# Reordered output steps, a PV product one head later, and earlier splits of weights and keys in a one-core attention and gating block

## The reference

```python
h = rmsnorm(x, norm_gain)
a_u, a_v, a_z, b_q, b_k, b_v, b_z, i_q, i_k, i_w = split_cols(h @ w_in, IN_SIZES)  # 3 x 512, 512, 64, 64, 512, 512, 64, 8
ya = spatial_gating(a_u, a_v, ...)           # gelu, layernorm of v, masked 128x128 mixing in blocks
q, k = rmsnorm(b_q per head, q_norm_gain), rmsnorm(b_k, k_norm_gain)
# per block of 128 queries (8 index heads, 8 attention heads, one shared k and v):
idx_score = sum over heads of relu(i_q . layernorm(i_k)) * i_w * scale
sel = top_k(where(admissible, idx_score, NEG), 256)     # ties: the earlier key
p = softmax(q . k[sel] * scale - slope[head] * |qpos - sel|, inadmissible = NEG)
yb = p @ v[sel]
# each branch is multiplied by silu(z) and normed by rmsnorm per branch or head
out = x + concat(ya, yb) @ w_out
```

## Time and profile before

| what | before |
|---|---|
| median of 3 runs | 565.14 us (564.82 to 565.28) |
| the profiled execution | 565.3 us |
| its span (first to last instruction) | 563.5 us |
| TensorE busy | 545.6 us, 97% |
| VectorE, ScalarE, GpSimd busy | 444.0, 371.5, 180.0 us |
| granted clock of TensorE, mean | 1.00 |

### The profile page before, as it was taken

How to read it: one execution, slowest core, us unless ns; L and a number is a source line. 1 busy time by engine, 2 the same in 40 slices (tenths; PEclk the granted TensorE clock), 3 DMA queues, 4 the chain that set the end, 5 groups by cost and what they waited for, 6 DMA issues and landing times. The chain is left out here.

```text
span 563.5 us, 8936 instructions
## 1 busy us (share of the span) xinstructions
PE 545.6 (97%) x2974; PEld 461.4 (82%) x2974; DVE 444.0 (79%) x1107; ACT 371.5 (66%) x711; POOL 180.0 (32%) x283
## 2 busy tenths in 40 slices
PE   8999999999999999999999999989999999999997
PEld 8997788878888888887888887768788789889886
DVE  4775777899889998999878888887878787866631
ACT  5885667767997767777988566756465555755510
POOL 1760000014449997667210003551112021202130
PEclk9999999999999999999999999999999999999999
DMA  8623110012331111131212144503030302011032
GB/s 250 214 66 110 57 38 20 1 38 76 112 93 39 38 46 49 39 94 39 56 58 74 52 133 134 170 19 95 19 94 20 94 19 76 20 40 35 1 113 75
DMA packets 39982, 39.69 MB, mean 70 GB/s; under 512 B 6144, under 2 KB 28160, under 8 KB 39936
## 3 DMA queue, kind: packets, MB, share of 16 engines
q1 hardware_dynamic: 38416, 39.11, 22.9%
q10 hardware_dynamic: 1520, 0.01, 0.1%
HBM read 30.72 MB, written 8.39 MB: 69 GB/s over the span
## 5 line engine op out<-in xcount | busy, mean ns | idle before, releaser
L1072 PE MATMUL ps_proj<-w_hi,xT_hi 128*128 128x512 f32 (+1 forms) x432 | 164.7, 381 | 1.2 <-DVE w_lo L1382 1.0
L1072 PE MATMUL ps_proj<-w_lo,xT_hi 128*128 128x512 f32 (+1 forms) x432 | 161.1, 373 | 0.0
L1072 PE MATMUL ps_proj<-w_hi,xT_lo 128*128 128x512 f32 (+1 forms) x432 | 161.1, 373 | 0.0
L912 ACT ACTIVATE ps_lg<-score,cand 128x768 f32<-128x768 f32 (+2 forms) x96 | 96.0, 1000 | 10.4 <-DVE cand L1475 10.4
L1072 PEld LDWEIGHTS ps_proj<-w_lo,xT_hi 128*128 128x128 f32 x432 | 81.4, 188 | 14.8
L1072 PEld LDWEIGHTS ps_proj<-w_hi,xT_hi 128*128 128x128 f32 x432 | 81.4, 189 | 14.5 <-DVE w_lo L1382 2.0
L1072 PEld LDWEIGHTS ps_proj<-w_hi,xT_lo 128*128 128x128 f32 x432 | 81.5, 189 | 11.8
L969 ACT CAST xT_hi<-ps_tp 128x512 fp32r<-128x512 f32 (+3 forms) x96 | 43.0, 483 | 66.0 <-PE ps_tp L1193 66.0
L1696 DVE TENSOR_TENSOR xT_lo<-ps_tp,xT_hi 128x512 fp32r<-128x512 f32 (+3 forms) x96 | 50.4, 553 | 31.4 <-ACT xT_hi L969 31.1
L1382 DVE SCALAR_TENSOR_TENSOR w_lo<-stage,g_in,w_hi 128x512 fp32r<-128x512 f32 x48 | 43.1, 905 | 10.0 <-ACT w_hi L772 9.2
L953 ACT ACTIVATE lo_f<-lo_f,negmax 128x128 f32<-128x128 f32 (+7 forms) x64 | 50.2, 785 | 0.2
(11 more groups left out here) (175 smaller groups left out, 1101.7 us busy)
## 6 DMA issues: line engine op xcount, KB each, us to landing
stage<-in_w_in_dram SPq DMA_DIRECT2D x48, 256.0 KB, 2.7
x_in<-in_x_dram SPq DMA_DIRECT2D x8, 512.0 KB, 6.0
lo_f<-in_x_dram SPq DMA_DIRECT2D x7, 512.0 KB, 4.0
out_dram<-lo_f SPq DMA_DIRECT2D x7, 512.0 KB, 3.5
q_scratch<-nat SPq DMA_DIRECT2D x8, 256.0 KB, 2.1
q_in<-q_scratch SPq DMA_DIRECT2D x8, 256.0 KB, 3.6
stage<-in_w_out_dram SPq DMA_DIRECT2D x8, 256.0 KB, 2.7
z_scratch<-nat SPq DMA_DIRECT2D x8, 256.0 KB, 2.1
```

What stands on the lines that cost most here:

```text
L912: act.activation(ps_lg[i % 2][:, 0:keys(t)], score[:, sc_off[t]:sc_off[t] + keys(t)], ACT.Sign, bias=cand[:, t:t + 1].bitcast(F32), scale= ...
L1072: mm = pe.matmul(ps_proj[u % 2][:, 0:n], a[:, k, rows], b[:, k, 0:n], start=(k == 0 and i == 0), stop=(k == KB - 1 and i == 2))
```

## The change

It moves work on all three engines and adds none. TensorE: the PV products of a pair run at the odd head m=2j+3 in place of the even 2j+2; the 16 output steps per tile are dealt out 3,2,3,2,2,2,1 over h=1 to 7 and 1 over h=0 in place of two each; `qiT` stands a block earlier for tiles 3 and up; the key transposes of tile 6 go into the first index projection. ScalarE: `copy_yT` one head later (h=1 and 5); `hi_w` of the last out weights up to one or two heads earlier (W_AT); the IQ weights one tile earlier. VectorE: `add_res` of the first half at h=3 in place of h=4 behind `lo_q`; late steps at other heads (LATE_AT by tile); the first q norm and the first counting round behind the sum of the heads of tile 7.

```diff
-    IQ_W_BEHIND = 2
+    IQ_W_BEHIND = 1
-        W_AT = (16, 16, 17, 17, 20, 21, 22, 23)
+        W_AT = (15, 15, 16, 17, 19, 20, 21, 22)
@@ ScalarE @@
-                if t > 0:
+                if 0 < t < T - 1:
                     hi_k(t - 1)
...
                 hi_w(KB + k)
+            hi_k(T - 2)
@@ ScalarE, attention @@
-                    if h == 0 and t > 0:
+                    if h == 1 and t > 0:
                         copy_yT(t - 1, 1)
-                    if h == 4:
+                    if h == 5:
                         copy_yT(t, 0)
@@ TensorE @@
-                    if k == 2 and t + 1 < T:
+                    if k == (2 if t <= T0 else 1) and t + 1 < T:
                         qiT(t + 1)
...
-                if t > 0:
+                if 0 < t < T - 1:
                     kT(t - 1)
+            def late_keys(k):
+                if k == 2:
+                    kT(T - 2)
...
-                    project(IQ, t)
+                    project(IQ, t, late_keys)
@@ TensorE, attention @@
-            STEPS = 2
-            assert STEPS * H == 2 * KB
+            STEPS = {1: 3, 2: 2, 3: 3, 4: 2, 5: 2, 6: 2, 7: 1, 0: 1}
+            assert sum(STEPS.values()) == 2 * KB
...
-                    steps = STEPS_BZ[m] if m < len(STEPS_BZ) else STEPS
+                    steps = STEPS_BZ[m] if m < len(STEPS_BZ) else STEPS[h]
...
-                    if m % 2 == 0 and m > 0:
+                    if m % 2 == 1 and m > 2:
                         pv(m // 2 - 1)
...
-            for _ in range(STEPS):
+            for _ in range(STEPS[0]):
                 next(pending)
@@ VectorE @@
-                if t > 0:
+                if 0 < t < T - 1:
                     lo_k(t - 1)
...
                 lo_w(KB + k)
+            lo_k(T - 2)
...
+                if t == 1:
+                    background(True, False)
+                    q_norm(0)
                 if t >= 2:
                     lo_w(KB * AV + t)
                 q_sums(t)
+                if t == 0:
+                    continue
                 background(True, False)
                 q_norm(t)
@@ VectorE, attention @@
-            LATE_AT = ((2, 4, 6), (2, 4, 6), (0, 2, 4, 6))
+            LATE_AT = ((2, 4, 6), (2, 4), (0, 2, 4, 6), (0, 2, 4, 6), (1, 3, 5, 7))
...
+                    if h == 3 and t > 1:
+                        add_res(t - 2, 0)
                     if h == Q_AT and t + 1 < T:
                         lo_q(t + 1)
-                    if h == 4 and t > 1:
-                        add_res(t - 2, 0)
...
-                    if h in LATE_AT[min(t, 2)]:
+                    if h in LATE_AT[min(t, 4)]:
                         next(late, None)
```

## The result

The changed kernel takes 589.66 us, the median of five runs from 587.0 to 590.2; the kernel before 565.2. The ratio is 1.042, with a 95% interval from 1.040 to 1.044. It is slower, by 24.5 us. The profiled execution took 590.2, its span 588.4.

What follows compares the result with a forecast made beforehand. TensorE, busy 97% of the span at clock 1.00, bounds the kernel, so only its idleness can change. Terms -1.3 -1.2 -1.4 -3.0 +22.2 -.1 = +15.2: 580.5 us profiled, 580.3 median; whole range 570 to 589.

Steps and rivals of the forecast that it cites:

- third rival: Clock falls to 1.2 GHz behind the longest waits, for one or two heads: 585 to 590; chance .09.
- first half: Before attention: tile 6 keys and indexer weights -1.3, qiT earlier -1.2, first q norm moved -1.4.
- tiles 0 to 3: Attention: waits go for copy of y, add_res and out weights, less costs at m=16 and q transposes; -3.0.
- tiles 4 to 7: Attention: even heads lose PV cover and late steps delay VectorE; +26.2 of waits less 4.0, net +22.2.
- at the end: End of kernel: one step fewer stands ahead of the last mix; -.1.
- the moved q norm: First half: VectorE does this work some 2.3 us later, absorbed by idle spots from 163 on; TensorE charged nothing.
- head 16: m=16: two weight splits ahead of the mix, no PV cover; +1.0, and +.5 for the PV group behind.
- at h=0: Tiles 4 to 7: transposes of P wait for the lo mix, 1.9, 2.8, 2.6 and 1.6; sum 8.9.
- at h=4: Tiles 4 to 6: transposes wait for lo_q behind a late step, 2.4, 4.0 and 1.8; sum 8.2.
- at h=2 and 6: Tiles 4 to 7: transposes wait for the bank that y_rows reads; sums 4.1 and 3.1.
- head 33's 1.9: m=32 and 33: PV pair 15 delays head 32's hi half and the exponential behind it; +1.9.
- what is given back: Tiles 4 to 7: today's waits, 1.2 on xT_lo and eight smaller, all go or are swallowed; 4.0 with late starts.

Runs made afterwards that it cites:

- e3: The kernel before with only the first-half edits (indexer weights, tile 6 keys, qiT, first q norm): 561.01 us, ratio .9919.
- e12: e3 with add_res ahead of lo_q at h=4 of tiles 2 and 3, two steps at every head kept: 561.0 us, ratio .9925.
- e5: e4 with two output steps at every head and add_res back behind lo_q at h=4: 560.9 us, ratio .9939.
- e10: e9 with the out weights of head 15 moved to head 16 (W_AT 16, 16, 16, 17, 19, 20, 21, 22): 566.93 us, ratio 1.0029.
- e11: e5 with W_AT 16, 16, 16, 17, 19, 20, 21, 22, the same out weights as e10: 563.27 us, ratio .9953.
- e1: The changed kernel with PV products back at even heads and copy of y at h=0 and 4; late steps stay odd: 573.82 us, ratio 1.0136.
- e2: The changed kernel with late steps of tiles 4 to 7 back behind even heads; PV stays at odd heads: 576.27 us, ratio 1.019.
- e8: e5 with both PV and the late steps of tiles 4 to 7 at odd heads: 588.53 us, ratio 1.0409.
- e4: The changed kernel with PV, copy of y and late steps all back where they were: 570.73 us, ratio 1.0091.
- e6: e5 with PV at odd heads and the copy of y one head later: 575.64 us, ratio 1.0178.
- e9: e4 with output steps dealt 3,2,3,1,2,1,2 over h=1 to 7 and 2 over h=0: 571.37 us, ratio 1.0095.
- e7: e5 with the late steps of tiles 4 to 7 behind odd heads: 565.73 us, ratio 1.0016.

## Why the prediction was right, and where it was off

Forecast +15.2, measured +24.9 in the profiled runs (565.3 to 590.2). Direction and mechanism were right. The size was not: the median of 589.66 lies .66 above the upper end of the range and 1.7 above the 588 of the main forecast, among the 585 to 590 of the third rival. The difference of 9.7 is, by parts: -.4 in the first half, +1.7 in tiles 0 to 3 and +2.0 in tiles 4 to 7 without the clock, +.1 at the end, and +6.4 for the four falls of the clock, which the sum had at nothing.

- *First half*, -3.9 forecast, -4.34 measured at the first scores, and confirmed by e3 alone. The first index logit is 1.2 earlier, and the last one 4.3. VectorE's lag from the moved q norm cost nothing that e3 shows.
- *Tiles 0 to 3*, -3.0 forecast, +.26 measured (-4.34 to -4.08), 1.6 of it a fall of the clock. This is the step that failed beside the clock. I took each wait of TensorE as a gain in itself. e12 takes two of them away, e5 the third (1.6 on w_lo), and neither is faster than e3. In e12 VectorE is full there, and the wait comes back at the next thing that is owed; in e5 1.61 are waited for at the mix of head 16 instead, and 1.93 in place of 1.08 for the accumulator. At head 16, which I had put at +1.0, TensorE waits 2.25. Two weight splits, 1.34 together, are ahead of the mix on ScalarE (without them the wait is 1.1 shorter, e10 and e11):

```profile
349.73 1.34 ACT L772 ACTIVATE w_hi<-hi_f,g_out 128x512 fp32r<-128x512 f32 x2
350.97 1.05 ACT L998 CAST mixT_hi<-ps_tp 128x512 fp32r<-128x512 f32 x2
```

and TensorE behind it:

```profile
352.41 0.52 PE L1199 MATMUL ps_tp<-ident,lo_f 128*128 128x128 f32 x3 [2.25 <-DVE xT_hi L1732]
```

- *Tiles 4 to 7*, +22.2 forecast, +29.0 measured; some 4.8 of this are three falls of the clock, and 24.2 the waits with their slow starts. By heads: at h=0 1.9, 2.8, 2.6 and 1.6 became .8 (and 1.1 just ahead, on the mix transposes, for which I had nothing), 2.46, 2.67 and 1.49; at h=4 2.4, 4.0 and 1.8 became 2.24, 3.71 and 1.63; at h=2 and 6 the sum of 7.2 became 5.3; head 33's 1.9 became 1.7. Of my 26.2 there are 22 of pure wait in these places, 23.7 of idleness in all, and about 2.9 of slower starts on top (estimated as the 7.7 of more busy time less 4.8), so 26.6. What I had wrong is what is given back: I took 4.0 for a wait of 1.2 and "eight smaller ones", but the kernel before is idle for only 2.35 in this stretch, with three waits above .2 (1.19, .28, .48). That is most of the 2.0. The reasons, the lost cover of PV and VectorE's queue with the late step ahead of the extra operations, are each shown by a removal (e1, e2), and that they cost more together than apart by e5 to e8.
- *The clock*, rival three with a chance of .09, was real: three falls there and one at head 16, 6.4 us. I had thought of it only at waits near 4 us; it fell after 2.24 in this kernel, after 1.84 in e4 (at 364.6), and in three of seven runs of e5, whose longest wait is 1.93 in the profiled run. Even the kernel before, whose longest wait is 1.65, had a mean clock of .996 or .997 and some 1 us more in 15 of the 49 runs that stand beside the experiments, so that its one trace at 1.00 said less than I took from it. The rule of "TensorE: Matmul & The Clock Gate", Part 1, of the Trainium skill, that idle gaps bring the clock back to half, agrees with these rows in kind. Which gaps do it, these runs don't settle: 2.67 here and 3.52 in e11 had no fall behind them.
- *One step less at h=7 and h=0* I counted as cover lost for the mix alone, inside the h=0 sum. e4 shows a cost of its own with PV at even heads, 9.8 us against e5 (1.2 of it the last store). With PV at odd heads it is .6 by the medians of e6 and e2, and 1.1 by those of e8 and the change: there the kernels with add_res at h=3 lack the waits of 2.3 and 1.6 for the second accumulator that e6 has, and wait about as much longer in other places. So two errors of opposite sign stand in the sum, and that they nearly cancel is luck.
- *VectorE's idleness ahead of L1708* I expected unchanged. It grew from 31.4 to 51.4 us (400 to 545 before, 400 to 570 after), nearly all of it waiting for ScalarE's hi half, which in turn waits for TensorE's transposes:

```profile
L1708 DVE TENSOR_TENSOR xT_lo<-ps_tp,xT_hi 128x512 fp32r<-128x512 f32 x42 | 28.4, 689 | 51.4 <-ACT xT_hi L970 50.9
```

What stays open: why the last store takes longer in some kernels; why one wait of 2.67, and in e11 one of 3.52, went without a fall where shorter ones had one, and why the same wait, of 1.86 in e9 and of 1.87 in e10, had a fall behind it in the one and not in the other; and what add_res at h=3 and the dealing of the steps are worth apart, since they weren't tried apart. No version beats the first half alone, 561.0 us (e3; e5 and e12 are the same within their spread).

## What to carry to other kernels

A long product on the leading engine is cover for whatever the others owe at that place; before it is moved, write down for each place the queue that ends there and the work that hides it, since two moves that each uncover a little (14.7 and 4.8 us here) uncover together more than their sum (27.6). Taking away a wait of the leading engine gave nothing where the engine that it waits for had no gap behind it (e12: 1.8 us of waits gone, 0.0 gained); look for the gap on that engine, and not only for the wait. And a wait of some 2 us may be paid for again when the clock falls behind it, here some 1.6 us each.

## What the runs showed of the hardware

Each fall of the granted clock to half inside a run's work lasted 3.4 us in the profiled runs. All but one of them began within 1.3 us of the end of a wait of TensorE of 1.6 to 3.7 us, one (e2, at 406.24) behind waits of only 1.09, .57 and .26 close together. Each cost 1.4 to 2.1 us in e5 and e6, and about 1 in the kernel before (565.97 to 566.72 at .996 and .997, against 565.03 to 565.83 at .999 and 1.00). Whether it fell changed from run to run of the same kernel (e5: four runs at 1.00, three at .997 and .994; the kernel before: 15 of 49 below .999). The four runs of e3, all at clock 1.00, spread by .16 us; those of e7, at 1.00 to .991, by 5.6.
